# The first query panel ahead of the next block's key panel in a hybrid decoder step

## The reference, cut to what matters

```
h  = h + mix @ w_out                    # output projection, 8 panels of 128 columns ("W")
r2 = rsqrt(mean(h*h) + eps)             # one number per token
q  = (h * g_cross) @ w_cq * r2          # cross-attention queries, 4 panels ("Q")
...                                     # scores, softmax, values, output ("O"), then the SwiGLU ("F")
k' = rmsnorm(x_next) @ w_in[:, K]       # of the next block: its key panel ("I", role k)
```

## Time and profile before

| what | value |
| --- | --- |
| three runs, us | 3242.48, 3246.65, 3249.24 |
| median of the runs | 3246.65 us |
| the profiled execution | 3245.05 us |
| its span in the profile | 3243.3 us |
| mean granted TensorE clock | 0.932 of full |

### The profile page before, as it was taken

The page is one execution under the profiler, slowest core; times in us unless marked ns, Lnnn a source line. Parts: engine busy times, 40 slices in busy tenths (PEclk is TensorE's granted clock), DMA queues, the critical chain, the costliest instruction groups (busy, mean ns, idle before and its releaser), DMA issues. The chain is left out here.

```text
span 3243.3 us, 35792 instructions
## 1 busy us (share of the span) xinstructions
PE 2996.9 (92%) x13972; PEld 2396.2 (74%) x13972; DVE 1484.3 (46%) x2221; ACT 1135.1 (35%) x1826; POOL 1027.3 (32%) x507
## 2 busy tenths in 40 slices
PE   7877999999999999999999999999779999667898
PEld 5656787877877878778778787788668888565742
DVE  5655655666346556553465566524352222313111
ACT  4542464345233543452346434422332222111100
POOL 3200433333444333334443333344224444410000
PEclk8988999999999999999999999999889999656679
DMA  4146423222335232223352222233313332571256
GB/s 132 53 116 155 136 72 89 71 72 79 98 107 166 72 88 72 72 79 97 107 167 78 85 72 66 85 97 114 107 40 97 98 98 91 152 210 45 64 183 222
DMA packets 490989, 332.44 MB, mean 103 GB/s; under 512 B 58559, under 2 KB 458051, under 8 KB 490806
## 3 DMA queue, kind: packets, MB, share of 16 engines
q1 hardware_dynamic: 486318, 323.74, 34.3%
q10 hardware_dynamic: 1880, 6.34, 0.5%
q0 software_dynamic: 2624, 0.09, 0.1%
HBM read 309.86 MB, written 21.23 MB: 102 GB/s over the span
## 5 line engine op out<-in xcount | busy, mean ns | idle before, releaser
L799 POOL TENSOR_TENSOR w_lo<-w_raw,w_hi 128x1024 fp32r<-128x1024 f32 x400 | 973.9, 2438 | 1717.6 <-ACT w_hi L813 1717.6
L1583 PE MATMUL L<-xa_h,w_hi 128*128 128x512 f32 x1536 | 613.2, 399 | 4.0 <-DVE xa_l L1402 4.0
L1584 PE MATMUL L<-xa_h,w_lo 128*128 128x512 f32 x1536 | 601.6, 392 | 0.0
L1585 PE MATMUL L<-xa_l,w_hi 128*128 128x512 f32 x1536 | 601.0, 391 | 0.0
L813 ACT ACTIVATE w_hi<-w_raw 128x1024 fp32r<-128x1024 f32 x400 | 421.1, 1053 | 437.6 <-PE L L1585 431.2
L1583 PEld LDWEIGHTS L<-xa_h,w_hi 128*128 128x128 f32 x1536 | 290.0, 189 | 75.1 <-issue 11.4
L1585 PEld LDWEIGHTS L<-xa_l,w_hi 128*128 128x128 f32 x1536 | 290.1, 189 | 61.6
L1584 PEld LDWEIGHTS L<-xa_h,w_lo 128*128 128x128 f32 x1536 | 290.4, 189 | 58.9 <-issue 1.0
L1542 DVE TENSOR_TENSOR sg<-sg,L 128x512 f32<-128x512 f32 x88 | 60.5, 688 | 531.4 <-PE L L1585 531.4
L1583 PE MATMUL L<-hid_h,w_hi 128*128 128x512 f32 x704 | 280.0, 398 | 6.1 <-DVE hT L1550 6.1
L1584 PE MATMUL L<-hid_h,w_lo 128*128 128x512 f32 x704 | 274.8, 390 | 0.0
(11 more groups left out here) (489 smaller groups left out, 4413.0 us busy)
## 6 DMA issues: line engine op xcount, KB each, us to landing
w_raw<-in_w_gate_dram SPq DMA_DIRECT2D x88, 512.0 KB, 3.8
w_raw<-in_w_up_dram SPq DMA_DIRECT2D x88, 512.0 KB, 3.8
w_raw<-in_w_down_dram SPq DMA_DIRECT2D x88, 512.0 KB, 3.4
w_raw<-in_w_in_dram SPq DMA_DIRECT2D x56, 512.0 KB, 3.8
xt<-xT_dram SPq DMA_DIRECT2D x48, 256.0 KB, 4.1
wS<-in_w_down_dram SPq DMA_DIRECT2D x11, 1024.0 KB, 4.9
wS<-in_w_gate_dram SPq DMA_DIRECT2D x10, 1024.0 KB, 5.1
wS<-in_w_up_dram SPq DMA_DIRECT2D x10, 1024.0 KB, 5.1
```

Of the source, the lines that this page charges most:

```text
L799: pool.tensor_tensor(w_lo[:, n % RING, 0:w], w_raw[:, n % RING, 0:w], w_hi[:, n % RING, 0:w].bitcast(F32), ALU.subtract)\
L1583: pe.matmul(acc, wh, rh, start=(k == 0), stop=False)
L1584: pe.matmul(acc, wl, rh, start=False, stop=False)
L1585: last = pe.matmul(acc, wh, rl, start=False, stop=(k == kn - 1))
```

## The change

In the order of the panels Q0 goes in front of the next block's key panel k. TensorE multiplies W7, Q0, then `token_sums`, then k, then `norm_rows`, then Q1 to Q3. Q0's result stays in its bank until `row_back` has the norm rows in SBUF. Since VectorE reads k's result before Q0's, a `read_order` sets the semaphore counts. On VectorE, `norm1_t` and `norm1_lo` of x tile 7 move behind `sum_squares` of panel 7; `token_rsqrt` and `diagonal` move ahead of the key panel's eviction; `row_back` stays behind it. On ScalarE the rounding of panel Q1 moves ahead of the key panel's slot. In the last block the order of the instructions is as it was.

```diff
@@ panel_order
         order += [("W", b, n) for n in range(KT)]
+        order += [("Q", b, 0)]
         if b + 1 < NBLK:
             order += [("I", b + 1, role) for role in WIN1]
-        order += [("Q", b, n) for n in range(CH)]
+        order += [("Q", b, n) for n in range(1, CH)]
@@ build
-            eng = "A" if by_act else "D"
-            counts[eng] += 1
-            ev_engine.append(eng)
-            ev_count.append(counts[eng])
+            ev_engine.append("A" if by_act else "D")
+
+    read_order = list(range(len(order)))
+    for n, (stage, b, i) in enumerate(order):
+        if stage == "Q" and i == 0 and order[n + 1][0] == "I":
+            read_order[n], read_order[n + 1] = n + 1, n
+    ev_count = [0] * NOUT
+    for n in read_order:
+        for m in range(panels[n][2]):
+            o = first_out[n] + m
+            counts[ev_engine[o]] += 1
+            ev_count[o] = counts[ev_engine[o]]
@@ ScalarE
+                    round_panel(pos[("Q", b, 0)] + AHEAD)
                     if more:
                         window(b + 1, WIN1)
                     for n in range(CH):
-                        round_panel(pos[("Q", b, n)] + AHEAD)
+                        if n >= 1:
+                            round_panel(pos[("Q", b, n)] + AHEAD)
                         act.wait_ge(s["ev_D"], ev_count[out_of("Q", b, n)])
@@ VectorE
-                        if more:
+                        if more and n < KT - 1:
                             for i in ahead:
                                 norm1_t(b + 1, i)
...
-                        if more:
+                        if more and n < KT - 1:
                             for i in ahead:
                                 norm1_lo(b + 1, i)
                     sum_squares(b, 0, KT - 1)
                     if more:
+                        norm1_t(b + 1, KT - 1)
+                        norm1_lo(b + 1, KT - 1)
+                    diagonal(token_rsqrt(b, 0))
+                    if more:
                         window(b + 1, WIN1)
-                    diagonal(token_rsqrt(b, 0))
                     row_back(b, 0)
@@ TensorE
+                    if not more:
+                        token_sums(b, 0)
+                    multiply(pos[("Q", b, 0)], a_rhs, lambda k: pe.wait_ge(s["n2_l"], KT * b + k + 1))
                     if more:
+                        token_sums(b, 0)
                         project(b + 1, WIN1[0])
-                    token_sums(b, 0)
-                    for n in range(CH):
-                        first = (lambda k: pe.wait_ge(s["n2_l"], KT * b + k + 1)) if n == 0 else None
-                        multiply(pos[("Q", b, n)], a_rhs, first)
-                        if n == 0:
-                            norm_rows(b, 0)
+                    norm_rows(b, 0)
+                    for n in range(1, CH):
+                        multiply(pos[("Q", b, n)], a_rhs)
```

More of the change, by code:

```diff
@@ L232, in out_of @@
         return first_out[pos[(stage, b, i)]] + m
-    bank_of, ev_engine, ev_count = [], [], []
+    bank_of, ev_engine = [], []
     counts = {"A": 0, "D": 0}
```

## The result

The changed kernel took 3264.26 us (median of 4 runs, 3261.43 to 3266.19) against 3245.89 us of the kernel before: a ratio of 1.0056, interval 1.0039 to 1.0073. Beside the experiments it was timed again, median of 5 runs: 3256.9 us against 3243.44, ratio 1.0042 (1.0029 to 1.0054). The change makes the kernel slower, by 13.5 to 18.4 us.

What follows compares the result with a forecast made beforehand. The prediction took PE, busy 92% of the span, as the bound. To 3245.05 us it added 8.2 for Q1's later starts and 5.1 for the clock, giving 3258.4, stated as 3258, range 3247 to 3267.

Steps and rivals of the forecast that it cites:

- The first wait: PE before Q0's last k-step: goes on 1.43 us earlier, leaving no wait in block 0, about 1.1 us in blocks 1, 2.
- The norm chain behind POOL: DVE's tiny instructions before `diagonal`: most run behind POOL's two `w_lo`, so `diagonal` starts 2.03 us after that pair ends.
- Q0's eviction on PE's path: Before Q1, which takes Q0's bank: Q1 starts 5.63 us after POOL's pair ends, later by 2.55, 2.78 and 2.91 us.
- The part called 8.2 us: Later start of Q1 in blocks 0 to 2, summed, without the clock's cost: 8.2 us.
- A: Time from W7's end to Q1's start, summed over blocks 0 to 2; Q1's later start was forecast at 8.2 us.
- B: Time from Q1's start to Q3's, two panels, summed over blocks 0 to 2; read from each profile.
- the term of the clock: PE around Q1, blocks 0 to 2: half clock behind two waits costs 1.7 us per block, 5.1 us; ends 0 and 9.6.
- No stall behind POOL: Rival: the norm chain passes POOL's `w_lo` or one holds it, hidden by the key panel; -1 us, 3244; chance 0.18.
- one `w_lo` in the way: Case of the not-slower rival: only one of POOL's `w_lo` delays the norm chain; +1 us, 3246.
- The clock stays: Rival: PE's waits cost 8.2 us but half-clock stretches fall into idle time; 3253 us; chance 0.22.
- Faster: Rival: all of PE's former waits and block 1's slow stretch go, some 10 us; 3235 us; chance 0.04.

Runs made afterwards that it cites:

- q2_round_late: The changed kernel, but ScalarE rounds panel Q2 behind `k_h` instead of ahead of it; 3244.3 us against 3242.7 of the kernel before, ratio 1.0012.
- own_bank: The changed kernel, but Q0's result gets bank 3 for itself in every block; 3254.7 us against 3242.7 of the kernel before, ratio 1.0029.
- q0_evicted_first: The changed kernel, but VectorE does `row_back` and Q0's eviction ahead of the key panel's eviction; 3259.6 us against 3243.4 of the kernel before, ratio 1.0050.
- filler: The changed kernel with unread matmuls in PE's two waits, 12 before `norm_rows` and 6 before Q1; 3248.4 us against 3242.7 of the kernel before, ratio 1.0020.
- before_own_bank: The kernel before in its old order, with bank 3 for Q0 and `norm_rows` behind Q1; 3245.8 us against 3243.4 of the kernel before, ratio 1.0005.
- own_bank_late_rows: The changed kernel with bank 3 for Q0 and `norm_rows` issued behind Q1; 3238.2 and 3237.0 us, ratios 0.9980 and 0.9977 to the kernel before.
- before_q2_late: The kernel before, but ScalarE rounds Q2 behind Q0's `cq_h`; 3242.5 us against 3243.4 of the kernel before, ratio 0.9995.

## Why the prediction was right

It gave 3258 us, 3247 to 3267, slower. Measured were 3264.3 and, beside the experiments, 3256.9. How near the medians come to 3258 says little: in the profile the changed part is 15.7 us longer where 13.3 were forecast, and the rest of the difference is the start of block 0.

**The first wait.** Forecast: none in block 0 and about 1.1 us in blocks 1 and 2, for `xa_l`. Measured: none, 1.15 and 1.19. Right.

**The norm chain behind POOL.** Forecast: L188 slips in, one instruction held by each `w_lo`, the rest behind the pair, `diagonal` at E + 2.03. Measured: just that, with `diagonal` at 375.25, E + 2.01 (E is the end of POOL's pair). q2_round_late shows for the second of the two instructions that the hold is the cause. E itself was forecast 11.85 us behind W7's end in block 0 and is 12.53, as DVE was further behind PE there.

**Q0's eviction on PE's path.** Forecast: Q1 at E + 5.63. Measured: 5.71 in block 0, but 6.65 and 6.05 in blocks 1 and 2. Here a step was short: it priced `norm_rows` at full clock, and the clock had fallen by then (2.08 and 1.48 us instead of 1.12). own_bank shows that the wait in front of Q1 is the bank's, and q0_evicted_first that the key panel's eviction costs nothing, as argued.

**The sizes.** The part called 8.2 us is A, and measured 10.1. Of the 1.9 us more, 1.3 are the two slow `norm_rows` and 0.4 is E (0.7 later in block 0, 0.15 earlier in each of the others). The clock was taken at 5.1 us: B rose by 6.4, with the 1.3 it makes 7.7, and filler gives 8.1 for it. So **the term of the clock was mis-sized**, by some 2.6 to 3 us. The prediction had all three blocks fall, as they did, but took 1.7 us for each because part of a stretch would lie over the second wait. In the profile 6.4, 5.3 and 4.4 us of half clock lie over work behind that wait, and half of their sum is 8.05: nearly the whole of each stretch cost its half. In sum A and B are 16.5 us longer where 13.3 were forecast. From W0 to W0 it is 15.7: the output projection came out 0.8 us shorter, which no run explains (in block 1 its length lies between 48.7 and 50.2 us over the twelve profiles), and from Q3 to the next block the sums agree, with two half-clock stretches there in either profile, in other places.

The rule of the Trainium skill that was weighed, page "TensorE: Matmul & The Clock Gate", section "Why this matters for your kernels" (long idle gaps between bursts of matmuls bring the lower clock back), agrees: granted clock 0.53, 0.50 and 0.51 behind the waits in the three blocks, and full clock there once filler took the idle time away.

**The rivals.** "No stall behind POOL" fell with the two held instructions. Its bound for one `w_lo` in the way was +1 us, and q2_round_late is that case. The median came to +1.6 us, but that nearness is luck: A alone is 3.4 us more and B 3.1, for the wait for Q0's eviction stayed at 1.64 us and the clock fell behind it in blocks 0 and 1. "The clock stays" fell. "Faster" would have needed Q1 not to wait for Q0's bank; with the bank free and the norm rows later the kernel is indeed faster.

What stays open: why the stretch ahead of block 0 ends up to 9 us earlier or later from one profile to the next. No run tried that. The two profiles of the changed kernel differ there by 8.0 us and the medians of their sets by 7.4 (those of the kernel before by 2.5), so it may go with the set of runs rather than with the single execution. As long as that is open, differences of a few us between medians count for less than A and B.

## What to carry to other kernels

Before an evacuation is put off to wait for something, look at who takes that bank next: with two banks in turn, putting off one result puts it in front of the next panel but one. Here that turned hidden work into a wait of 1.6 us per block. A third bank took that wait away, but the order paid only when `norm_rows` was moved behind Q1 as well. A chain of tiny VectorE instructions must not be placed by its own length alone: here each `w_lo` of GpSimd beside it held one instruction of 0.16 us for up to 2.3 us. And a wait on PE costs more than its length when the clock falls behind it; between before_own_bank and own_bank_late_rows the waits became 4.4 us shorter and the stretches 7.8.

## What the runs showed of the hardware that was not expected

Idle waits of the same length on PE are followed by a half-clock stretch in one execution and not in another: the 2.6 us for `xb_l` in block 2 had none behind it in the kernel before, 3.4 us in before_own_bank and 6.6 us in before_q2_late. In the kernel before, that wait and the busy time by stretch behind it:

```profile
1659.95 0.50 PE L1583 MATMUL L<-xb_h,w_hi 128*128 128x512 f32 x1 [2.59 <-DVE xb_l L1135]
```

```profile
1660.00:1665.40 5.40, 5.40 (x28) 4.60 (x29) 5.16 (x7) 1.86 (x4) 4.92 (x2) 1.00 0.38 85
```

The same in before_own_bank:

```profile
1662.00:1665.40 3.40, 3.40 (x9) 2.63 (x8) 3.17 (x6) 0.68 (x1) 3.17 (x2) 0.50 0.44 94
```

Over all profiles the clock fell within 2.5 us behind 5 of 6 waits of 2.6 us for `xb_l` in blocks 1 and 2, behind 1 of 16 waits of 1.2 us for `xa_l`, and behind all 9 pairs of waits around `norm_rows` in the two profiles of the changed kernel and in q0_evicted_first. More work on PE made a kernel faster: 54 matmuls that nobody reads took 8.1 us out of the stretches around Q1, and the median went from 13.5 (in one set of runs) to 5.7 us above the kernel before (in another). The falls are worth as much as the edits under study: two edits that removed waits of 1 to 1.6 us as expected (before_own_bank and before_q2_late) showed no gain in the median.
